# The second up-projection of a two-block transformer: one k-pair by seven products, its halves turned through HBM

## What is computed

```python
def conv_gated_ffn(h, w_up, conv_w, conv_b, w_down):
    u = h @ w_up                                   # (256, 2048) @ (2048, 2 * 5632)
    up_ = jnp.pad(u, ((0, 0), (1, 1), (0, 0)))
    u = up_[:, :-2] * conv_w[0] + up_[:, 1:-1] * conv_w[1] + up_[:, 2:] * conv_w[2] + conv_b
    gate, val = jnp.split(u, 2, axis=-1)
    return (jax.nn.silu(gate) * val) @ w_down
...
    x = x + conv_gated_ffn(rms_norm(x, norm2_g), w_up, conv_w, conv_b, w_down)
```

## Time and profile before

| | |
|---|---|
| median of 3 runs | 2124.8 us (2124.76 to 2128.15) |
| the profiled execution | 2125.52 us, its span 2123.4 us |
| PE | 2108.5 us busy, 99% of the span |
| PE weight loads | 1753.0 us, 83% |
| DVE | 1738.8 us, 82% |
| ACT | 1194.7 us, 56% |
| POOL | 80.4 us, 4% |
| moved by DMA | 404.81 MB, mean 191 GB/s |
| FF2, turns 0 to 10 | from about 1405 to 1886 us of the span |

### The profile page before, as it was taken

How to read it: one execution, slowest core, us unless ns; L and a number is a source line. 1 busy time by engine, 2 the same in 40 slices (tenths; PEclk the granted TensorE clock), 3 DMA queues, 4 the chain that set the end, 5 groups by cost and what they waited for, 6 DMA issues and landing times.

```text
span 2123.4 us, 28090 instructions
## 1 busy us (share of the span) xinstructions
PE 2108.5 (99%) x9682; PEld 1753.0 (83%) x9682; DVE 1738.8 (82%) x2498; ACT 1194.7 (56%) x1562; POOL 80.4 (4%) x114
## 2 busy tenths in 40 slices
PE   9999999999999999999999999999999999999999
PEld 7897888888888888888889878888888888888887
DVE  5889977888888887979766557569999999999787
ACT  6556675555555545545466446556666666665454
POOL 1000000001000100000000042000000000000000
PEclk9999999999999999999999999999999999999999
DMA  7665355677767767566556544466666666656665
GB/s 225 197 181 169 111 181 155 214 231 231 224 208 227 237 213 242 191 215 199 173 164 173 169 115 152 148 184 187 194 191 185 199 188 194 190 184 199 210 198 178
DMA packets 219710, 404.81 MB, mean 191 GB/s; under 512 B 14335, under 2 KB 58953, under 8 KB 219371
## 3 DMA queue, kind: packets, MB, share of 16 engines
q1 hardware_dynamic: 215755, 391.13, 59.5%
q0 software_dynamic: 3696, 11.54, 1.7%
q10 hardware_dynamic: 176, 1.06, 0.1%
HBM read 395.80 MB, written 7.86 MB: 190 GB/s over the span
## 4 chain that ended last, share of the span: by engine, by line
PE 82%; DVE 11%; issue 4%; ACT 2%; DMA 0%; DVEq 0%; ACTq 0%; POOL 0%; POOLq 0%
PE ps L679 20%; PE ps L681 20%; PE ps L680 20%; PE ps L985 6%; PE ps L986 6%; PE ps L987 6%; DVE w_lo L2075 3%; DVE gate_T L2128 2%; DVE val_T L2128 1%; PE ps L717 1%; ACT w_hi L1398 1%; DVE stage L2941 1%; DVE stage L2949 1%; DVE cv L2187 1%; PE ps L741 0%
## 5 line engine op out<-in xcount | busy, mean ns | idle before, releaser
L2075 DVE TENSOR_TENSOR w_lo<-raw,w_hi 128x1024 fp32r<-128x1024 f32 (+2 forms) x701 | 837.7, 1209 | 210.5 <-ACT w_hi L1398 204.0
L1398 ACT ACTIVATE w_hi<-raw 128x1024 fp32r<-128x1024 f32 (+2 forms) x701 | 724.6, 1045 | 459.2 <-PE ps L681 348.3
L679 PE MATMUL ps<-w_hi,hT_hi 128*128 128x512 f32 (+2 forms) x1792 | 699.8, 390 | 3.0 <-DVE w_lo L2075 2.3
L681 PE MATMUL ps<-w_hi,hT_lo 128*128 128x512 f32 (+2 forms) x1792 | 690.6, 385 | 0.0
L680 PE MATMUL ps<-w_lo,hT_hi 128*128 128x512 f32 (+2 forms) x1792 | 690.3, 385 | 0.0
L679 PEld LDWEIGHTS ps<-w_hi,hT_hi 128*128 128x128 f32 x1792 | 336.6, 188 | 72.7 <-DVE w_lo L2075 6.9
L681 PEld LDWEIGHTS ps<-w_hi,hT_lo 128*128 128x128 f32 x1792 | 336.4, 188 | 63.2
L680 PEld LDWEIGHTS ps<-w_lo,hT_hi 128*128 128x128 f32 x1792 | 336.8, 188 | 59.8
L679 PE MATMUL ps<-w_hi,aT_hi 128*128 128x512 f32 x480 | 187.1, 390 | 0.8 <-DVE w_lo L2075 0.8
L681 PE MATMUL ps<-w_hi,aT_lo 128*128 128x512 f32 x480 | 186.8, 389 | 0.0
L680 PE MATMUL ps<-w_lo,aT_hi 128*128 128x512 f32 x480 | 186.7, 389 | 0.0
(11 more groups left out here) (391 smaller groups left out, 2324.0 us busy)
## 6 DMA issues: line engine op xcount, KB each, us to landing
raw<-in_w_up SPq DMA_DIRECT2D x264, 512.0 KB, 4.2
raw<-in_w_down SPq DMA_DIRECT2D x176, 512.0 KB, 4.7
raw<-in_w_gate SPq DMA_DIRECT2D x88, 512.0 KB, 3.8
raw<-in_w_in SPq DMA_DIRECT2D x80, 464.0 KB, 3.7
raw<-in_w_out SPq DMA_DIRECT2D x64, 512.0 KB, 4.0
raw<-in_w_in SPq DMA_DIRECT2D x64, 256.0 KB, 3.2
raw<-in_w_in SPq DMA_DIRECT2D x24, 448.0 KB, 3.5
turn_rows<-stage POOLq DMA_DIRECT2D x11, 512.0 KB, 5.0
```

Source lines behind the costliest of these rows:

```text
L679: pe.matmul(o, xh, wh, start=first, stop=False)
L681: mm = pe.matmul(o, xl, wh, start=False, stop=last)
L1398: act.activation(w_hi[:, s, :kc, :width], raw[:, s, :kc, :width], ACT.Copy).then_inc(hi_ready, 1)
L2075: dve.tensor_tensor(w_lo[:, s, :kc, :width], raw[:, s, :kc, :width], w_hi[:, s, :kc, :width].bitcast(F32), ALU.subtract).then_inc(lo_ready, 1)
```

## The change

In turns 1 to 10 of FF2 the k-pair 7 of gate and value (now tiles 7 and 8, `UP_ORDER`) becomes a unit of seven products (`up_seven`); turn 0 and the other pairs stay. Three matmuls of 128x512 less are issued in such a turn. DVE and ACT get FF1's steps for it: `up_combine`, `up_combine_rest`, `up_unit_hi`, `up_extra`, `up_value_add`, once each. `turn_strips` goes: `copy2` writes the gate into the second and the value into the third third of `stage`, `up_blocks` transposes the blocks into the first, POOL stores it and reads it back into the third it came from, and `strips2` (ACT) makes `gate_T` or `val_T` of it. There are two such trips a turn. The combinations `up_comb`, `up_comb_hi` and `up_comb_lo` lie where `x_sb` lies; POOL stores x into `x_rows` before turn 1 and fetches it after the value of turn 10 is complete, before the down-projection's extra products are added to it.

```diff
              (1, 1), (1, 2), (1, 3), (1, 4), (1, 5)]
 FF1_UNIT = [5, 9]
+UP_ORDER = [(0, i) for i in range(8)] + [(1, 7)] + [(1, i) for i in range(7)]
+UP_UNIT = 7
+UNITS1 = len(FF1_UNIT) * (FB - 1)
 HELD = 8
 DN_GROUP = [T_DN1, T_DN1B, T_DN2, T_DN2 + 2 * DN_PAIRS]
...
         ss = sb("ss", [P, 64])
+        up_comb_hi, up_comb = overlay([("up_comb_hi", [P, 4, NB], F32R), ("up_comb", [P, 4, NB], F32)])
+        up_comb_lo = overlay([("under_up_comb", [P, 4, NB], F32), ("up_comb_lo", [P, 4, NB], F32R)])[1]
         x_sb = sb("x_sb", [P, TOK, DM])
         raw = sb("raw", [P, RING, 2, NB])
...
+            ("up_s_hi", [P, 4, P], F32R), ("up_s_lo", [P, 4, P], F32R)])[1:]
         aT_hi = sb("aT_hi", [P, FC, SEQ], F32R)
         aT_lo = sb("aT_lo", [P, FC, SEQ], F32R)
...
-        raw_s = gate_s
+        up_rows = [stage[:, 1 + i].rearrange("p c s -> p (c s)").rearrange("p (t n) -> p t n", t=TOK) for i in range(2)]
         prod_T = stage[:, 2].rearrange("p c s -> p (c s)")
         turn_out = stage[:, 0].rearrange("p c s -> p (c s)")
         turn_rows = nc.dram_tensor("turn_rows", (3, P, 4 * SEQ), F32, kind="Internal").ap()
+        x_rows = nc.dram_tensor("x_rows", (P, TOK * DM), F32, kind="Internal").ap()
         cg, cval = stage[:, 1], stage[:, 2]
         a_s = attn1[:, :, 0:NB]
...
-                load_block(T_FF2, 16 * j, w_up2, [2] * 8, cols(j))
-                load_block(T_FF2 + 8, 16 * j, w_up2, [2] * 8, cols(j + FB))
+                for n, (half, i) in enumerate(UP_ORDER):
+                    load(T_FF2 + n, 16 * j, [w_up2, w_up2[:, :, DFF:]][half], 2 * i, cols(j))
             for q in (2, 3):
                 group_loads(q, w_down2, 2 * q - 4)
...
                     rotate(2)
                     rotate(3)
+                if name == "x3":
+                    pool.dma_start(x_rows, x_sb[:].rearrange("p t n -> p (t n)")).then_inc(x_saved, 16)
+                    with pool.Fori(1, FB + 1) as j:
+                        for half in range(2):
+                            pool.wait_ge(turned, FB + 2 * j - 1 + half)
+                            pool.sem_inc(pool_seen)
+                            pool.dma_start(turn_rows[half], turn_out).then_inc(turn_saved, 16)
+                            pool.wait_ge(turn_saved, 16 * (FB + 2 * j - 1 + half))
+                            pool.sem_inc(pool_seen)
+                            strips_back(half, stage[:, 1 + half].rearrange("p c s -> p (c s)"))
+                    pool.wait_ge(ff_value, 2 * (FB - 1))
+                    pool.dma_start(x_sb[:].rearrange("p t n -> p (t n)"), x_rows).then_inc(x_back, 16)
 
 
...
+                pe.wait_ge(lo_ready, c + 1 + 16 * j)
+                three(ps[:, 4, :], a11, b11, True, True)
+                three(ps[:, 0, :], a12, b21, False, True).then_inc(tile_used, 1)
+                pe.wait_ge(gemm_free[1], G_FF2 + j)
+                pe.wait_ge(lo_ready, c + 2 + 16 * j)
+                three(ps[:, 2, :], sums[3], b22, True, False).then_inc(tile_used, 1)
+                pe.wait_ge(ff_split, 2 * UNITS1 + 2 * j - 1)
+                three(ps[:, 7, :], sums[0], comb[0], True, True)
+                three(ps[:, 6, :], sums[1], comb[1], True, True).then_inc(ff_used, 1)
+                pe.wait_ge(ff_split, 2 * UNITS1 + 2 * j)
+                three(ps[:, 5, :], sums[2], comb[2], True, True)
+                three(ps[:, 1, :], a22, comb[3], False, True).then_inc(ff_used, 1)
...
+            pe.wait_ge(ff_sums_split, 2)
             with pe.Fori(1, FB) as j:
                 pe.wait_ge(gemm_free[0], G_FF2 + j)
-                ff_tiles(T_FF2, 16 * j, 0, 0, 8)
-                pe.wait_ge(gemm_free[1], G_FF2 + j)
-                ff_tiles(T_FF2 + 8, 16 * j, 1, 0, 8)
+                for n in range(UP_UNIT):
+                    gemm_tile(T_FF2 + n, 16 * j, H, 2 * n, pair(0), n == 0, False)
+                up_seven(j)
+                for n in range(UP_UNIT + 2, 16):
+                    up_value_tile(n, j)
...
-            def copy2(j, half):
-
-                act.wait_ge(tile_used, T_FF2 + 8 + 8 * half + 16 * j)
+            def copy2(j, half, added=False):
+
+                if not added:
+                    act.wait_ge(tile_used, T_FF2 + 8 + 8 * half + 16 * j)
+                elif half:
+                    act.wait_ge(ff_value, FB - 1 + j)
+                else:
+                    act.wait_ge(ff_added, FB - 1 + j)
+                    act.wait_ge(aT_ready, j)
                 for t in range(TOK):
-                    ins = act.activation(raw_s[:, t, :], ps[:, 2 * half + t, :], ACT.Copy, scale=r_of(rstd, "x3", t, 1))
+                    ins = act.activation(up_rows[half][:, t, :], ps[:, 2 * half + t, :], ACT.Copy, scale=r_of(rstd, "x3", t, 1))
                 ins.then_inc(gemm_free[half], 1)
+
+            def strips2(j, half, dst):
+
+                act.wait_ge(turn_back, 64 * (FB + 2 * j + 1 + half))
+                act.activation(by_strip(dst[:].rearrange("p c s -> p (c s)")),
+                               stage[:, 1 + half].rearrange("p c s -> p (c s)").rearrange("p (i m a) -> p i m a", i=4, a=32),
+                               ACT.Copy).then_inc(value_turned if half else gate_turned, 1)
...
+            def up_turn(j, after):
+
+                hi_tiles(T_FF2, 16 * j, 0, 4)
+                copy2(j - 1, 1, after)
+                hi_tiles(T_FF2, 16 * j, 4, 5)
+                strips2(j - 1, 0, gate_T)
+                hi_tiles(T_FF2, 16 * j, 5, 6)
+                center2(j - 1, 0)
+                hi_tiles(T_FF2, 16 * j, 6, 8)
+                up_unit_hi(j)
+                hi_tiles(T_FF2, 16 * j, 9, 10)
+                silu2(j - 1)
+                hi_tiles(T_FF2, 16 * j, 10, 11)
+                act.wait_ge(ff_used, 2 * UNITS1 + 2 * j)
+                act.activation(up_comb[:, 0, :], ps[:, 4, :], ACT.Copy).then_inc(ff_copied, 1)
+                hi_tiles(T_FF2, 16 * j, 11, 12)
+                strips2(j - 1, 1, val_T)
+                center2(j - 1, 1)
+                hi_tiles(T_FF2, 16 * j, 12, 14)
+                hidden_hi(j - 1)
+                hi_tiles(T_FF2, 16 * j, 14, 15)
+                copy2(j, 0, True)
+                hi_tiles(T_FF2, 16 * j, 15, 16)
...
                     dve.wait_ge(first_copied, q + 1)
+                    if q == 2:
+                        dve.wait_ge(x_back, 16)
...
+            def up_blocks(half):
+
+                for t in range(TOK):
+                    out = turn_out.rearrange("p (q c t a) -> p t c q a", q=4, c=4, t=TOK)[:, t]
+                    ins = dve.transpose(out, up_rows[half][:, t, :].rearrange("p (c q b) -> p c q b", c=4, q=4))
+                ins.then_inc(turned, 1)
...
+                dve.tensor_tensor(t1, raw[:, sb_, 0, :], raw[:, sa, 0, :], ALU.subtract)
+                dve.tensor_tensor(t3, raw[:, sb_, 1, :], raw[:, sb_, 0, :], ALU.subtract).then_inc(ff_ready, 1)
+                dve.wait_ge(ff_ready, 2 * UNITS1 + 2 * j - 1)
+                dve.tensor_tensor(t2, raw[:, sb_, 1, :], t1, ALU.subtract).then_inc(ff_step, 1)
+                dve.wait_ge(ff_step, 4 * (FB - 1) + 3 * j - 2)
+                dve.tensor_tensor(t4, raw[:, sa, 1, :], t2, ALU.subtract).then_inc(ff_ready, 1)
...
+                if part == 0:
+                    dve.wait_ge(ff_copied, FB - 1 + j)
+                    dve.tensor_tensor(u2, ps[:, 5, :], u1, ALU.add).then_inc(ff_step, 1)
+                    dve.tensor_tensor(ps[:, 0, :], ps[:, 0, :], u1, ALU.add)
+                    dve.wait_ge(ff_step, 4 * (FB - 1) + 3 * j - 1)
+                    dve.tensor_tensor(u4, ps[:, 7, :], u2, ALU.add)
+                    dve.tensor_tensor(u3, ps[:, 6, :], u2, ALU.add).then_inc(ff_step, 1)
+                else:
+                    dve.wait_ge(ff_step, 4 * (FB - 1) + 3 * j)
+                    dve.tensor_tensor(u2, ps[:, 7, :], u3, ALU.add)
+                    dve.tensor_tensor(ps[:, 1, :], ps[:, 1, :], u3, ALU.add).then_inc(ff_added, 1)
...
+                dve.wait_ge(tile_used, T_FF2 + 16 + 16 * j)
+                dve.wait_ge(ff_added, FB - 1 + j)
+                dve.tensor_tensor(ps[:, 2, :], ps[:, 2, :], up_comb[:, 3, :], ALU.add)
+                dve.tensor_tensor(ps[:, 3, :], ps[:, 3, :], up_comb[:, 1, :], ALU.add).then_inc(ff_value, 1)
...
+            def up_turn(j, after):
+
+                lo_tiles(T_FF2, 16 * j, 0, 3)
+                if after:
+                    up_value_add(j - 1)
+                lo_tiles(T_FF2, 16 * j, 3, 5)
+                dve.wait_ge(gemm_free[1], G_FF2 + j)
+                dve.wait_ge(turn_saved, 16 * (FB + 2 * j - 1))
+                up_blocks(1)
+                lo_tiles(T_FF2, 16 * j, 5, 6)
+                taps2(j - 1, 0, parts=(0,))
+                lo_tiles(T_FF2, 16 * j, 6, 7)
+                taps2(j - 1, 0, parts=(1,))
+                up_combine(j)
                 lo_tiles(T_FF2, 16 * j, 7, 8)
+                up_combine_rest(j)
+                lo_tiles(T_FF2, 16 * j, 9, 11)
+                up_extra(j, 0)
```

(32 more changed lines are left out.)

126 lines of the change are left out of this document (82 added, 44 removed).

## The result

The changed kernel takes 2192.2 us (median of 4 runs, 2190.2 to 2196.3), the kernel before, run beside it, 2124.8. The ratio is 1.0317, with an interval of 1.0298 to 1.0337: 67 us slower. The forecast was 33 us slower (2158, range 2138 to 2175). Sign and mechanism came as told, but the loss is twice the forecast. The profiled execution took 2196.33 us around a span of 2194.6, so its span is 71.2 us above that of before.

A forecast was written before the change was run, and what follows sets the result against it. TensorE's matmuls were taken to bound the kernel, with DVE close behind in FF2. Turn 1 +0.6, turns 2 to 10 +30.8 and the last down projection's start +1.7 add 33.1 to 2124.8: 2158 us, range 2138 to 2175.

The forecast's parts named there:

- Part 1: FF2 turns 1 to 10, tiles 7 and 8: 21 matmuls instead of 24, at best 0.84 us a turn gained.
- Part 3: FF2 behind the unit: TensorE waits 0.7 us each for tiles 12 and 13, together 1.45 a turn.
- the ring: In FF2 the gate's trip, the splits to tile 7, the unit and the next gate's blocks form a 47.1 us loop.
- Part 4: FF2 gate's trip through HBM delays tile 5's split and all behind it: 47.1 us a turn instead of 43.68.
- The trip: Gate from POOL's store until the last strip lands: 5.4 + 1.65 + 4.9 = 11.95 us, from FF1.
- Rival C: In FF2 two trips a turn beside the weights get slower: 14 us each, turn 48.6, 2171 us; chance 0.10.
- the 0.60: From the end of DVE's gate blocks to POOL's issue of the store: 0.60 us, read in FF1.
- The unit: The seven products' 21 matmuls on TensorE, right after the wait for tile 7: 4.76 us, taken as 4.8.
- The head: Start of the last down projection: last gate back late, eight taps ahead of tile 6's split, +1.7 us.
- part 5: Nearly free items: the value's trip hidden behind 20 us, storing x taken as 0, fetching x back 0.
- Storing x: POOL's store of x ahead of turn 1: cost between 0 and 3 us, taken as 0.
- The sum: Turn 1 +0.6, turns 2 to 10 +30.8, start of the last down projection +1.7: together +33.1 us.

## Why the prediction was half right

**Part 1 (three matmuls fewer).** Right: 9652 for 9682. It is no longer what a turn is made of.

**Part 3 (behind the unit).** Right. In the turn shown the first add stands at T9 + 0.83 (1675.63, with T9 at 1674.80, 0.20 ahead of ACT's copy); tile 12 starts at 1683.60, 0.64 late, and tile 13 at 1687.07, another 0.75, together 1.39 for 1.45. The order alone was worth 1.24 us a turn once the ring was open. The prediction used it only for turn 1, and rightly left it out of the closed ring.

**Part 4 (the ring).** The mechanism is shown four ways: waits where they were foretold; the loss gone for the most part when the gate's use moved (45.5 us a turn) and wholly when the unit was left out (43.6); and the parts of the rest the same in every turn, to a few hundredths of a microsecond, while the trip varies by 3 us. The steps that failed are two terms of its sum, both too small.

- *The trip, 11.95 from the store's issue.* It was read in FF1. In FF2 it measured 13.63: 5.95 to the first strip for 5.4, and 7.68 to `gate_T` for 6.55. 1.7 us in each of nine turns is 15 us. Rival C had this as "the trips get slower because there are now two a turn beside the weights" and put 0.10 on 14 us with the 0.60 ahead; the measured 13.63 + 0.60 = 14.2 is that rival's trip. Its reason is not shown: the value's store isn't what does it, and beside the raw loads no run tells.
- *The unit, "4.8".* It was priced at the full clock though the same paragraph made TensorE wait 2.7 us right in front of it. It took 6.52 in the turn shown; over nine turns the rest of the ring is 1.5 us longer, 14 us, and the low stretches account for 13 of it (8 x 1.6). No rival had it. The windows of the earlier trace rows have the clock at 1.00, but the trace of before holds one such fall, far ahead of FF2, right behind a wait of TensorE:

```profile
207.87 0.49 PE L843 MATMUL ps<-qkT 128*128 128x128 f32 x2 [1.94 <-ACT qkT L1537]
```
```profile
208.30:211.70 3.40, 3.40 (x13) 2.78 (x12) 2.71 (x9) 2.76 (x6) 0.00 (x0) 0.56 0.54 154
```

That row could have given the price, half of some 3.4 us. That a new wait for TensorE may cost a second time was the missing step.

With both, 9 x (50.30 - 43.68) = 59.6 where the sum had 30.8.

**The head, 1.7.** It measured 10.4. Only tile 6's place had been priced. The prediction took the last value's trip as hidden, but the head has no 20 us of matmuls to hide it behind the last splits, and **part 5**'s "fetching x back: 0" looked at when x is wanted and not at the raw tiles that share the DMA engines when it is issued. Moving both brought 6 us back; which share is whose is shown only for the fetch, 1.6 us or more. **Storing x**, in the same part, was right at 0: issued at 1427.99, landed in 9.1 us, ahead of turn 1.

**The sum.** 1.9 (chance start) + 59.6 (turns 2 to 10) - 0.7 (what is left over for turns 0 and 1, +0.6 foretold) + 10.4 = 71.2, for 33.1. The range went up only as far as rival C's own time (2171, 2174 with the storing of x), though the text calls that half of it; the trip took all of that room, and the clock and the head came on top.

## What to carry to other kernels

When a change closes a ring through DMA, price each link in the stage where it will stand, and ask of each link that is TensorE's whether it comes right behind a wait, for then it may run at half the clock. A trip of 13 us hurts only by what is queued behind its wait on an in-order engine: here moving one wait behind the unit's splits was worth 38 us, all the other edits together 22. And a saving of 3 matmuls in 192 is gone once the order of VectorE's work can't reach the ceiling within 0.84 us a turn.

## What the hardware showed

TensorE's granted clock fell to 1.2 GHz in eight of nine turns though no wait of its matmuls in the loop was longer than 2.5 us. In the turn shown the low stretch began 1 us into the work behind the wait, on the critical matmuls; 3.4 us of it cost 1.6, and the same stretch behind tile 5, where TensorE had to wait later anyway, cost the ring nothing. Five matmuls a turn (1.13 us) whose result nobody reads, put into the wait, went with one such stretch in place of eight. And a store of 512 KB took 6.65 us beside DMA engines 95% busy and 2.88 at 44%, in the same turn. Six DMAs of GpSimd in place of four for the same bytes lengthened the issue by 1.03 us.
